# A fused transformer-style layer pair on one core: eight modulation sums on VectorE, and a thinner spread of work between the gathers

## The reference

```
mod = silu(c) @ w_mod + b_mod              # 1024 x 6144; six vectors of 1024
sh1, sc1, gt1, sh2, sc2, gt2 = split(mod)
h  = rmsnorm(x, g1) * (1 + sc1) + sh1
x  = x + gt1 * (mixer(h @ w_in) @ w_out)    # three kinds of attention, a short convolution
h2 = rmsnorm(x, g2) * (1 + sc2) + sh2
# PEER: q = h2 @ w_q; scores against 2 x 128 keys for each of 8 heads; top 16 of 16 x 16 sums
# -> 128 experts a token, with softmax weights g
act = gelu(dot(h2, expert_u[e]))            # for each token and each of its 128 experts
x  = x + gt2 * sum_e g * act * expert_v[e]
x  = rmsnorm(x, ln_final)
# second block: rmsnorm, x @ w_in_2, causal attention with rotary positions, a gated delta rule, output
```

## Time and profile before

| what | us |
|---|---|
| median of three runs | 1398.9 |
| lowest, highest | 1396.18, 1405.27 |
| the profiled execution | 1404.89 |
| its span, first to last instruction | 1403.1 |
| PE, DVE, ACT, POOL busy in it | 1154.9, 743.8, 485.0, 363.9 |

### The profile page before, as it was taken

One profiled execution on the slowest core, in us unless ns is written; L12 is line 12 of the kernel. 1 busy time (PEld: TensorE's weight loads), 2 busy tenths in 40 slices (PEclk: granted clock), 3 DMA queues, 4 the chain that ended last, 5 costly groups with the idle time before them and its releaser, 6 DMA issues.

```text
span 1403.1 us, 15272 instructions
## 1 busy us (share of the span) xinstructions
PE 1154.9 (82%) x5688; PEld 673.4 (48%) x5688; DVE 743.8 (53%) x1808; ACT 485.0 (35%) x1282; POOL 363.9 (26%) x285
## 2 busy tenths in 40 slices
PE   6999968878787678666677766779988998999997
PEld 2888653332342123111122211134867887899883
DVE  5132658888639994465444455430466567642111
ACT  1131124463424452344332233321577544113101
POOL 0888013333334543333343334300000000000000
PEclk9989967998898999899999998889999999999999
DMA  9965418999999999999999999914413131114130
GB/s 392 326 260 212 162 71 324 361 351 401 396 412 421 415 418 394 415 421 422 422 394 405 395 396 421 422 69 181 180 61 117 63 121 62 62 61 180 60 120 31
DMA packets 57094, 378.70 MB, mean 270 GB/s; under 512 B 7187, under 2 KB 10428, under 8 KB 11964
## 3 DMA queue, kind: packets, MB, share of 16 engines
q0 software_dynamic: 36864, 268.45, 47.2%
q1 hardware_dynamic: 19488, 107.23, 20.2%
q10 hardware_dynamic: 668, 2.04, 0.4%
HBM read 376.64 MB, written 1.06 MB: 269 GB/s over the span
## 4 chain that ended last, share of the span: by engine, by line
PE 51%; DMA 21%; DVE 17%; ACT 7%; issue 3%; POOL 1%; ACTq 0%; POOLq 0%; DVEq 0%
PE ps L88 51%; DMA AR<-in_puv,idx 20%; DVE AR L88 8%; DVE RT L88 3%; ACT L88 2%; ACT av L88 1%; DVE rowb L88 1%; DVE hT L88 1%; DVE acc L88 1%; POOL AR L88 1%; DMA X<-in_x 1%; ACT acc L88 1%; ACT rowb L88 1%; DVE junk L88 1%; ACT AR L88 1%
## 5 line engine op out<-in xcount | busy, mean ns | idle before, releaser
L88 PE MATMUL ps<-AR,acc 128*64 128x512 f32 x912 | 355.5, 704 | 172.0 <-ACT acc L88 171.0
L88 POOL DMA_INDIRECT AR<-in_puv,idx x256 | 271.3, 1060 | 491.7 <-PE ps L88 395.9
L88 PE MATMUL ps<-hT,W 128*128 128x256 f32 (+1 forms) x1472 | 318.0, 374 | 4.2 <-ACT rowb L88 3.0
L88 PEld LDWEIGHTS ps<-hT,W 128*128 128x128 f32 x1472 | 268.5, 198 | 54.7 <-issue 15.4
L88 PEld LDWEIGHTS ps<-AR,acc 128*64 128x64 f32 x912 | 85.9, 150 | 414.1 <-ACT acc L88 335.3
L88 DVE CUSTOM_DVE_ANT_0 AR<-AR,mixT 128x1024 f32<-128x1024 f32 x128 | 156.9, 1228 | 155.1 <-DMA AR<-in_puv,idx 154.9
L88 DVE CUSTOM_DVE_ANT_0 AR<-AR,tok 128x1024 f32<-128x1024 f32 x128 | 153.0, 1220 | 58.4 <-DMA AR<-in_puv,idx 58.3
L88 ACT ACTIVATE av<-av 128x1 f32<-128x1 f32 x256 | 51.3, 200 | 314.2 <-DVE av L88 314.0
L88 ACT ACT_TABLE_LOAD x104 | 133.4, 1283 | 12.8 <-DVE PT L88 11.0
L88 PE MATMUL ps<-W,hT 128*128 128x512 f32 (+3 forms) x288 | 98.0, 498 | 0.8 <-ACT hT L88 0.8
L88 ACT ACTIVATE acc<-fold,av 128x64 f32<-128x64 f32 x228 | 79.3, 348 | 7.4
(11 more groups left out here) (231 smaller groups left out, 1092.3 us busy)
## 6 DMA issues: line engine op xcount, KB each, us to landing
W<-in_w_in SPq DMA_DIRECT2D x50, 1024.0 KB, 6.9
W<-in_w_mod SPq DMA_DIRECT2D x24, 1024.0 KB, 11.7
W<-in_w_out SPq DMA_DIRECT2D x4, 1024.0 KB, 5.9
W<-in_wq SPq DMA_DIRECT2D x4, 1024.0 KB, 8.1
AR<-in_puv,idx POOLq DMA_INDIRECT x256, 11.3
W<-in_wba SPq DMA_DIRECT2D x4, 1024.0 KB, 6.1
W<-in_wbb SPq DMA_DIRECT2D x4, 1024.0 KB, 7.0
W<-in_wo SPq DMA_DIRECT2D x4, 1024.0 KB, 6.0
```

The lines of the kernel that those rows point to most:

```text
L88: ins = f(*args, **kw)
```

## The change

It has five parts.

1. `mod_sum_v` takes the place of `mod_sum`: a TENSOR_SCALAR and seven SCALAR_TENSOR_TENSOR of 128 x 512 on VectorE. Slabs 10 and 11 are summed in the prologue too, so there are eight such sums, and `plan` and the calls are in a new order.
2. gt2 is then made as columns, with eight more one-column matmuls, and spread to R_G2 by `spread_g2` (four 128 x 128 matmuls and a copy, twice) in place of `load_row(3)` and `mod_row`.
3. Of the first 24 pairs, every fourth (p = 3, 7, ... 23) has no step of half1. The routing advances 5 parts a pair below pair 17 (before 6), 6 below pair 32 (before 8) and 8 after.
4. `x2_steps` takes both sums of squares on ScalarE and forms the second norm from them without waiting for the first; a half of 512 columns starts when its own bank is done. `qk_project` of tokens 0 to 127 becomes sixteen pieces of two matmuls (`qk_piece`), one a pair from pair 72 on, and `rope` follows them.
5. Matmuls that read hT wait for the k-tile that they read, not for all eight.

```diff
-        for (a, n), m in zip(((0, 512), (512, 512), (1024, 280), (1304, 512), (1816, 512), (2328, 512)), (6, 7, 8, 9, 4, 5)):
-            plan += [(w_in, a, n), (w_mod, m * 512, 512)]
+        cuts = [(w_in, a, n) for a, n in ((0, 512), (512, 512), (1024, 280), (1304, 512), (1816, 512), (2328, 512))]
+        mods = [(w_mod, m * 512, 512) for m in (6, 7, 8, 9, 4, 5, 10, 11)]
+        plan += [cuts[0], mods[0], mods[1], cuts[1], mods[2], cuts[2], mods[3], cuts[3], mods[4], mods[5],
+                 cuts[4], mods[6], cuts[5], mods[7]]
         plan += [(w_out, 0, 512), (w_out, 512, 512), (wq, 0, 512), (wq, 512, 512)]
-        for n in (10, 11):
-            plan.append((w_mod, n * 512, 512))
...
-        def mod_sum(buf, free):
+        def mod_sum_v(buf):
 
             i, w, t_w = next_w()
-            gtt = nc.gpsimd.tensor_tensor
-            t = G(gtt, w[:, :, :], w[:, :, :], cs.unsqueeze(2).to_broadcast([P, 8, 512]), MUL, after=[t_w, t_cs])
-            t = G(gtt, w[:, 0:4, :], w[:, 0:4, :], w[:, 4:8, :], ADD, after=[t])
-            t = G(gtt, w[:, 0:2, :], w[:, 0:2, :], w[:, 2:4, :], ADD, after=[t])
-            t = G(gtt, buf, w[:, 0, :], w[:, 1, :], ADD, after=[t] + free)
-            done_w(i, t)
-            return t
+            t = V(ts_, buf, w[:, 0, :], cs[:, 0:1], None, MUL, after=[t_w, t_cs])
+            for k in range(1, 8):
+                t = V(stt, buf, w[:, k, :], cs[:, k:k + 1], buf, MUL, ADD, after=[t])
+            return i, t
...
+        def spread_g2(n, after):
+
+            b = ps.take()
+            for j in range(4):
+                t = PE(mm, b.t[:, j * 128:j * 128 + 128], g2c[:, 4 * n + j:4 * n + j + 1].to_broadcast([P, P]), ident,
+                       start=True, stop=True, after=b.old + [t_g2c])
+            e = A(act, R_G2[:, n * 512:n * 512 + 512], b.t[:, :], ACT.Copy, after=[t] + after)
+            b.free = [e]
+            t_g2.append(e)
...
+        def of_k(t_r, k):
+            return t_r[k:k + 1] if len(t_r) == 8 else t_r
...
-                       after=b.old + [t_w] + t_r)
+                       after=b.old + [t_w] + of_k(t_r, k))
...
-        ms_buf = [RT[:, 512 * n:512 * n + 512] for n in range(3)] + [R_POST[:, 0:512], R_POST[:, 512:1024], R_LNF[:, 0:512]]
+        ms_buf = [RT[:, 512 * n:512 * n + 512] for n in range(3)] + [R_POST[:, 0:512], R_POST[:, 512:1024], R_LNF[:, 0:512]] + [R_G2[:, 512 * n:512 * n + 512] for n in range(2)]
...
-        mod_next()
+        done_w(*mod_next())
+        done_w(*mod_next())
 
         i, w, t_w = next_w()
+        third = mod_next()
...
+            if n == 2:
+                done_w(*mod_next())
...
-                    mod_next()
+                if (n, j2) == (0, 1):
+                    done_w(*sixth)
+                elif j2 == 0 and n < 2:
+                    done_w(*mod_next())
                 run_step(2)
+                if (n, j2) == (0, 0):
+                    sixth = mod_next()
...
+        for n in range(2):
+            t_mg2 = mod_cols_sum(b2, 16 + 4 * n, *t_ms[6 + n])
         attn_add(0, 1)
         norm_root(("c", 1), nrm[:, 1, :], cbT[:, :, P:2 * P], t_oc[1])
         q_norm1(0)
-        sh2, sc2, t_m2 = mod_affine(b2, t_mc[3], 24, V_LNF, 16)
+        sh2, sc2, t_m2 = mod_affine(b2, t_mg2, 24, V_LNF, 16)
+        g2c = modc[:, 32:40]
+        t_g2c = V(tt_, g2c, b2.t[:, 16:24], PV[:, V_BMOD + 40:V_BMOD + 48], ADD, after=[t_mg2, t_pc])
...
-                t = V(tt_, junk[:, c], E[a][n].t[:, :], R_G2[:, c], MUL, after=[t_acc] + t_g2 + ([t] if n else free))
+                t = V(tt_, junk[:, c], E[a][n].t[:, :], R_G2[:, c], MUL, after=[t_acc[n]] + t_g2 + free)
                 E[a][n].free = [t]
                 yield
                 t = V(tt_, X[:, a, c], X[:, a, c], junk[:, c], ADD, after=[t])
+                t_sum.append(A(act, PT[:, 1, 0:512], X[:, a, c], ACT.Square, accum_out=sums[:, 0, n:n + 1], after=[t] + x2_sq[0]))
+                x2_sq[0] = t_sum[-1:]
                 yield
-            r1, r2 = st[:, 14 + a:15 + a], st[:, 16 + a:17 + a]
-            t = V(ttr, junk[:, :], X[:, a, :], X[:, a, :], 1.0 / D, EPS, MUL, ADD, r1, after=[t])
-            t = A(act, r1, r1, ACT.Sqrt, after=[t])
+                t = V(tt_, junk[:, c], X[:, a, c], R_LNF[:, c], MUL, after=[t, t_rows[0]])
+                t_sum.append(A(act, PT[:, 1, 512:1024], junk[:, c], ACT.Square, accum_out=sums[:, 1, n:n + 1], after=[t] + x2_sq[1]))
+                x2_sq[1] = t_sum[-1:]
...
+            t_tot = V(tt_, tot, sums[:, :, 0], sums[:, :, 1], ADD, after=t_sum)
+            t = V(ts_, e, tot[:, 0:1], EPS / D, EPS * EPS, MUL, ADD, after=[t_tot])
+            t = V(stt, q, tot[:, 1:2], 1.0 / D, e, MUL, ADD, after=[t])
+            t = A(act, q, q, ACT.Sqrt, after=[t])
             yield
-            t = V(rec, r1, r1, after=[t])
+            t = V(rec, q, q, after=[t])
             yield
-            t_x2[a] = V(stt, X[:, a, :], X[:, a, :], r1, R_LNF, MUL, MUL, after=[t, t_rows[0]])
+            t_xb2[a] = V(ts_, tok2[:, a, :], junk[:, :], q, None, MUL, after=[t, t_lastdot[a]])
             yield
-            t = V(ttr, junk[:, :], X[:, a, :], X[:, a, :], 1.0 / D, EPS, MUL, ADD, r2, after=[t_x2[a]])
-            t = A(act, r2, r2, ACT.Sqrt, after=[t])
+            t = V(ts_, r, tot[:, 0:1], 1.0 / D, EPS, MUL, ADD, after=[t_tot])
+            t = A(act, r, r, ACT.Sqrt, after=[t])
             yield
-            t = V(rec, r2, r2, after=[t])
+            t = V(rec, r, r, after=[t])
             yield
-            t_xb2[a] = V(ts_, tok2[:, a, :], X[:, a, :], r2, None, MUL, after=[t, t_lastdot[a]])
+            t_x2[a] = V(ts_, X[:, a, :], junk[:, :], r, None, MUL, after=[t] + t_sum)
...
+        def qk_piece(kind, n, k0, free):
+            if (kind, n) not in wqk:
+                wqk[kind, n] = next_w()
+            i, w, t_w_ = wqk[kind, n]
+            if k0 == 0:
+                qk_bank[kind, n] = ps.take()
+            b = qk_bank[kind, n]
+            for k in (k0, k0 + 1):
+                t = PE(mm, b.t[:, :], hT[:, k, 0:P], w[:, k, :], start=(k == 0), stop=(k == 7),
+                       after=b.old + [t_w_, t_hb[0][k]])
+            if k0 == 6:
+                e = A(act, rot[kind, 0][:, n * 512:n * 512 + 512], b.t[:, :], ACT.Copy, after=[t] + free)
+                b.free = [e]
...
-            for todo_ in h1:
-                for f in todo_:
-                    f()
-                break
-            advance(routes[0], 6 if p < 17 else 8)
+            if p > 23 or p % 4 < 3:
+                for todo_ in h1:
+                    for f in todo_:
+                        f()
+                    break
+            advance(routes[0], 5 if p < 17 else 6 if p < 32 else 8)
...
-                load_row(3, [t_idx[1, 7], t_gw[1, 7]])
-                for n in range(2):
-                    t_g2.append(mod_row(3, n))
+                spread_g2(0, [t_idx[1, 7], t_gw[1, 7]])
+            elif len(routes) == 3 and len(t_g2) < 2:
+                spread_g2(1, [t_idx[1, 7], t_gw[1, 7]])
...
-            if p in (86, 92, 98, 104):
-                m = (p - 86) // 6
-                qk_project("qk"[m % 2], 0, m // 2, [t_tp, t_gw[1, 7]])
-            if p == 112:
-                rope("q", 0, [])
+            if t_hb and len(qk_done) < 16:
+                m, k0 = divmod(len(qk_done), 4)
+                qk_done.append(qk_piece("qk"[m % 2], m // 2, 2 * k0, [t_tp, t_gw[1, 7]]))
+            elif len(qk_done) == 16:
+                qk_done.append(None)
+                rope("q", 0, [t_x2[0]])
...
-        for _ in x2_steps(1, t_pelast, t_rot["k", 0]):
-            pass
+        last = x2_steps(1, e, t_rot["k", 0])
+        while t_xb2[1] is None:
+            advance(last, 1)
```

More of the change, by code:

```diff
@@ L449, in build @@
         done_w(i, t)
-        mod_next()
+        done_w(*third)
         t_B = flip_bias()
@@ L813, in q_project @@
                     t = PE(mm, b.t[:, j * 128:j * 128 + 128], w[:, k, q * 128:q * 128 + 128], hT[:, k, c],
-                           start=(k == 0), stop=(k == 7), after=b.old + [t_w] + t_hx[a])
+                           start=(k == 0), stop=(k == 7), after=b.old + [t_w, t_hx[a][k]])
             if js[-1] == 0:
@@ L1050, in build @@
         scores_add(4)
-        routes = [route(0, [])]
+        routes = [route(0, [t_mg2])]
         advance(routes[0], 1)
@@ L1200, in combine @@
                                 after=[e, t_fold] + dg_free[d] + ([late_t["dg"]] if "dg" in late_t else t_mc))))
+            ends = []
             for c in range(2):
@@ L1209, in combine @@
                         ring.append([n, [e]])
-            return e
-        ahead = []
+                ends.append(e)
+            return ends
+        ahead, qk_done = [], []
         h1 = half1()
@@ L1245, in build @@
                 routes.append(None)
-                load_row(3, [t_idx[1, 7], t_gw[1, 7]])
-                for n in range(2):
-                    t_g2.append(mod_row(3, n))
+                spread_g2(0, [t_idx[1, 7], t_gw[1, 7]])
```

(7 more changed lines are left out.)

23 lines of the change are left out of this document (16 added, 7 removed).

## The result

| | before | after |
|---|---|---|
| median of 20 runs, us | 1401.4 | 1409.2 |
| lowest and highest, us | 1395.9, 1408.7 | 1401.4, 1413.4 |
| profiled execution and its span, us | 1404.9, 1403.1 | 1405.9, 1404.1 |

The ratio of after to before is 1.0048, 95% interval 1.0033 to 1.0062: 6.7 us slower. The forecast was 1393, with a range of 1375 to 1408.

What follows compares the result with a forecast made beforehand. TensorE's chain bounds prologue and tail, the five-buffer ring the early pairs, DMA bytes the plateau. Prologue +9.5, bytes -10.8, pieces -6.8, early pairs +3.5, end -1.1 sum to -5.7 us: median 1398.9 becomes 1393, range 1375 to 1408.

Steps and rivals of the forecast that it cites:

- the clock: Prologue: a new TensorE standstill may bring another stretch at the lower granted clock; +1 us, between 0 and 8.5.
- The early pairs: Gather loop to pair 20: same chores and routing spread over 20 pairs, -2; with late indices +3.5 us, range -8 to +9.
- rival (a): Five-buffer stretch of the gather loop runs near its own lap, so the pauses pay: -11 us more, 1382; chance 0.26.
- the late indices: Gather loop: gathers wait for later head indices; +4 us for head 1 at pair 8, +1.5 for heads 2 and 3.
- The standstills in the prologue: TensorE waits for VectorE's third sum before w_in's third slab, +4.7 us, and for the seventh, +2 us.
- the columns: Prologue: eight more columns for gt2 stand in TensorE's path; +1.8 us.
- Rival (b): TensorE is stopped in the prologue, each standstill bringing a stretch at the lower clock: +16 us, 1409; chance 0.12.
- The bytes: Plateau, pairs 54 to 59: two slabs and one row less are loaded; -10.8 us.
- rival (c): Saved loads give nothing because VectorE's later routing sets the pace: +10.8 us, 1404; chance 0.10.
- The pieces: Pairs 86 to 114: two-matmul pieces remove the dips behind 16 records of qk_project; -6.8 us.
- the end: Last norm: reworked norm -0.3 us, and starting on the first k-tile saves 0.81; -1.1 us together.
- the signs: New profile: first gather near 211.5 us, wrong before 206 or after 218; first to last dot some 693 us.

Runs made afterwards that it cites:

- e9: Kernel before with only the change's last part: queries and keys in two-matmul pieces, new norm, waits by k-tile; ratio to before 0.9891.
- e4: Changed kernel with e1's old gather-loop order and e3's later third and seventh sums together; 1385.3 us, ratio to before 0.9879.
- e3: Changed kernel with the third and seventh sums written later, behind the additions and copies they stood ahead of; ratio to before 0.9978.
- e1: Changed kernel with the old gather-loop order: a chore behind every pair, six route parts to pair 16, then eight; 1393.6 us, ratio to before 0.995.
- e5: Changed kernel without the pauses alone: an attention chore behind every pair, route parts still five, six, eight; ratio to before 0.9989.
- e12: e5 with six route parts a pair up to pair 7, then five, six and eight; ratio to before 0.9949.
- e8: e4 with w_in and w_mod slabs loaded strictly in turn up to the fourth, then sums in pairs; ratio to before 0.9872.
- e13: e9 plus the two gt2 slabs loaded in the prologue ahead of w_out, summed on VectorE in other places; ratio to before 0.984.

## Why the prediction was wrong

The runs split the change into four parts. Each measured value is a quotient of two ratios, or the mean of two such quotients, and is uncertain by 3 to 6 us; that they add up to the whole follows from how they are formed.

| part | forecast, us | by which runs | measured, us |
|---|---|---|---|
| pieces, norm, waits by k-tile | -6.8 - 1.1 = -7.9 | e9 | -15.3 |
| early slabs, sums on VectorE, columns; no standstills | -10.8 + 1.8 = -9.0 | e4/e9 | -1.7 |
| the two standstills, with the clock | 4.7 + 2 + 1 = +7.7 | after/e3, e1/e4 | +9.9 |
| order of the gather loop | +3.5 | after/e1, e3/e4 | +13.9 |
| sum | -5.7 | | +6.8 |

**The early pairs are the step that failed, in its first half.** "They are the same work now, but spread over 20 pairs", with 20 x 5.2 + 17 = 121 us and "-2", took the 17 us of excess for all of the work, a fixed sum that thins out. It is not. The kernel before already told it: its pairs 15 to 20 took 33.5 us from first dot to first dot, 8.6 over the plateau's 24.9, where I put "some 3", since chores and routing go on behind pair 15. The 20 pairs took 128.8 us there. With the pauses, the three profiles have 135.4 to 138.0 us for them; without, all others have 124.6 to 132.9. Timed, the pauses cost 8.3 us (e5) where the forecast has a gain of 2, and that is the whole error of the row. The chores that they postpone hold up what follows: the second half's routing began behind pair 38's dots instead of pair 32's (VectorE waits 6.18 us for its first key scores at 472.31) and ended at 60 instead of 54, and pairs 32 to 41 took 56.0 us for 52.7. That this is where the 8.3 go is argued, not shown. That postponed steps come back was the forecast's own argument against rival (a), and it should have given the pauses a cost.

The second half of that step, the late indices, came out. The forecast named 9 us of dry DMA; POOL waited 8.55 at pair 8 and 4.78 at pair 16. I took "+4" for head 1 and "+1.5" for heads 2 and 3, 5.5 together, and e12, which frees all of them, shows 5.6, give or take 4.

**The standstills in the prologue** were right in their mechanism. The slab landed at 70.6 (forecast 71.7), the sum took 5.96 us (5.9), TensorE waited. Against e3, the changed kernel starts the columns 7.9 us later (179.81 for 171.95), as the forecast's 7.7 has it: 2.8 from the third sum (forecast 4.7; in e3 TensorE waits 2.35 us for the slab, so those are the load order's), 2.6 from the seventh (2), 2.5 from the clock behind it (1). Against the first and the second profile of the kernel before, the third slab starts 3.6 and 4.8 us later (forecast 4.7), the columns start 8.6 and 11.5 us later, so that the seventh sum and the clock cost 5.0 and 6.7 (forecast 2 + 1), and the first dot is 12.0 and 16.4 us later, so that the columns cost 3 to 5 (forecast 1.8). The clock is a mis-sized term: e3, without the standstills, has 1.00 in 130 to 160 us in place of 0.92. It falls at the columns too, which no term had: 24 records took 4.91 us, while 24 of the same shape took 2.73 just ahead of them. That need not be the standstills' doing, since e8, without them, has 4.71 there. Rival (b) is the one whose time came out, 1409, but of its 16 us above the forecast the standstills gave 2 and the loop's order 10.

**The bytes** came as forecast from pair 54 to 59 (-10.7), which speaks against rival (c). But "-10.8" counts only what leaves the loop, and the forecast set no more than +1.8 for the columns against it. This is the second step that failed: -9.0 forecast and -1.7 measured, with 6 us of doubt. What took the gain back, in e4 against e9, lies for the most part in the prologue, where the first dot comes 7.8 us later: 3.0 is there when the third slab starts (74.15 for 71.12, behind one more slab in line), 1.8 in the 16 records behind that wait (5.38 us for 3.62), and 2.9 is added from the first columns to the transposes (9.1 for 6.3 us). Another 2.2 us lie in pairs 0 to 41 and 1.8 behind the last dot, within what single profiles scatter. e13 regains part of it, but it also has six sums back on GpSimd and the old load order, so that place, order and engine are not told apart.

**The pieces** came in the trace where forecast (-6.1 from pair 86 to 114), but were worth 9.8 timed; **the end** was 2.4 us shorter on average of the two profiles, not 1.1, and with the waits by k-tile 5.5 timed, with 6 us of doubt. That these two were forecast too small hid more than half of the loop's error. Why the pieces give more than their stretch of the trace shows is open. Of the signs, the first gather came at 214.0, within 206 to 218 but later than 211.5, and the stretch from the first to the last dot took 699.4 us and not 693. Last, the forecast stood on a median of three runs; with 20 it is 2.5 us higher.

## What to carry to other kernels

Work that moves to an idle engine costs by the instruction behind which it is queued: list, for each place, what the next consumer is waiting for, and write the sum behind it. A loop that lives on a ring of buffers has no slack to postpone into: thinning its side work cost 8.3 us here, and slower routing, which delays the indices that the gathers need, another 5.6. And a bundle of edits is best split early, since here one part alone (e9, 1386 us) beat the whole (1409), and of the rest the early slabs paid only in other places (e13, 1380).

## What was not expected of the hardware

A wait on TensorE inside a dense stretch was followed by a lower granted clock: behind 7.07 and 5.64 us the clock was 0.86 and 0.82 in 76 to 92 us in the two profiles of the changed kernel, 1.00 before. Shorter waits had the same price: behind 2.35 us in e3 and 2.82 in e4 the 16 records took 5.38 us, as against 5.24 behind 7.07 and 6.03 behind 5.64. The Trainium skill (TensorE: Matmul & The Clock Gate, "HAM oscillation — how this bites in real kernels") says a wait for data can do this; the trace agrees, and the price here was 1.6 to 2.4 us of the 16 records (3.62 without a wait) and 2.5 of the 32 behind the seventh sum. The clock also fell where TensorE did not wait: the 8 column records of the kernel before took 1.74 and 1.03 us in its two profiles, at a granted clock of 0.54 and 1.00.

The first VectorE instruction of a sum beside GpSimd took 1.88 us in e13 where it took 0.49 alone, and ended at 138.61, as GpSimd's addition ended at 138.33. The Trainium skill (SBUF — State Buffer, "SBUF: two separate sides") calls the pair of ports that the two engines share an exclusive lock, held for a whole instruction; this row agrees, as far as GpSimd's rough spans tell. Taking GpSimd's sums away freed such waits in the changed kernel (3.99 us for a 128x4 product before), but nothing there was waiting for them.
